# Loading the scale columns of the modulation first and computing two 512-token projection jobs inside the modulation's load

## What is computed

```python
sh_x, sc_x, gt_x = split(silu(c) @ w_ada + b_ada, 3)        # 2048 wide each
sh_c, sc_c, gt_c = split(silu(c_ctx) @ w_ada + b_ada, 3)
h_x = rms_norm(x, norm_g) * (1 + sc_x) + sh_x               # 256 tokens
h_c = rms_norm(ctx, norm_g) * (1 + sc_c) + sh_c             # 256 context tokens
px = h_x @ w_in ;  pc = h_c @ w_in                          # 2048 x 6976
```

## Time and profile before

| | |
|---|---|
| median of 3 runs | 2210.15 us (2209.24 to 2214.47) |
| profiled execution, own time | 2212.03 us, its span 2210.2 us |
| PE busy | 2169.6 us, 98% of the span |
| PEld busy | 1797.2 us, 81% |
| DVE / ACT busy | 1422.2 us / 999.0 us |
| DMA | 409.23 MB, mean 185 GB/s |
| first tile of the first job starts / its eighth ends | 53.34 us / 133.25 us |

### The profile page before, as it was taken

How to read it: one execution, slowest core, us unless ns; L and a number is a source line. 1 busy time by engine, 2 the same in 40 slices (tenths; PEclk the granted TensorE clock), 3 DMA queues, 4 the chain that set the end, 5 groups by cost and what they waited for, 6 DMA issues and landing times.

```text
span 2210.2 us, 29923 instructions
## 1 busy us (share of the span) xinstructions
PE 2169.6 (98%) x11250; PEld 1797.2 (81%) x11250; DVE 1422.2 (64%) x2126; ACT 999.0 (45%) x1486; POOL 105.3 (5%) x124
## 2 busy tenths in 40 slices
PE   5999999999999999999999999999999999999999
PEld 1587888897778888888778888888888888888887
DVE  2257665646846676787788545687778787654455
ACT  3243233434545444555466445544444444344453
POOL 1020100102110120000000000000000000000000
PEclk8999999999999999999999999999999999999999
DMA  9976665543045666665413565666656666656674
GB/s 372 382 231 203 204 212 182 166 121 103 10 169 174 210 202 192 178 186 173 149 39 95 179 192 182 212 190 187 191 181 191 187 190 190 204 190 190 190 242 165
DMA packets 209908, 409.23 MB, mean 185 GB/s; under 512 B 15501, under 2 KB 24069, under 8 KB 208264
## 3 DMA queue, kind: packets, MB, share of 16 engines
q1 hardware_dynamic: 205536, 386.71, 55.3%
q0 software_dynamic: 3360, 16.76, 2.6%
q10 hardware_dynamic: 904, 4.29, 0.5%
HBM read 400.49 MB, written 7.22 MB: 184 GB/s over the span
## 4 chain that ended last, share of the span: by engine, by line
PE 89%; DVE 5%; DMA 3%; ACT 1%; issue 1%; POOL 0%; SPq 0%; DVEq 0%; ACTq 0%
PE bank L2088 52%; PE bank L2098 19%; PE bank L2104 10%; DMA ada_ring<-in_w_ada 2%; PE bank L2216 1%; PE bank L2328 1%; PE bank L2315 1%; PE bank L2274 1%; DVE wlo L1286 1%; PE bank L2240 1%; DMA raw<-in_w_out 1%; PE bank L2225 1%; PE bank L2506 0%; DVE st L1492 0%; DMA raw<-in_w_in 0%
## 5 line engine op out<-in xcount | busy, mean ns | idle before, releaser
L2088 PE MATMUL bank<-whi,xhl 128*128 128x512 f32 (+2 forms) x3776 | 1136.8, 383 | 4.7 <-DVE wlo L1286 3.0
L1286 DVE TENSOR_TENSOR wlo<-raw,whi 128x1024 fp32r<-128x1024 f32 (+2 forms) x649 | 773.1, 1204 | 465.1 <-ACT whi L776 443.6
L776 ACT ACTIVATE whi<-raw 128x1024 fp32r<-128x1024 f32 (+2 forms) x649 | 664.1, 1047 | 671.2 <-PE bank L2088 345.6
L2088 PEld LDWEIGHTS bank<-whi,xhl 128*128 128x128 f32 x3776 | 695.5, 188 | 141.9 <-DVE wlo L1286 6.6
L2088 PE MATMUL bank<-wlo,xhl 128*128 128x512 f32 (+2 forms) x1888 | 719.8, 381 | 0.0
L2098 PE MATMUL bank<-xhl,whi 128*128 128x512 f32 x1792 | 449.1, 392 | 0.0
L2088 PEld LDWEIGHTS bank<-wlo,xhl 128*128 128x128 f32 x1888 | 354.4, 188 | 67.3
L2098 PEld LDWEIGHTS bank<-xhl,whi 128*128 128x128 f32 x1792 | 322.3, 189 | 58.0 <-issue 0.3
L2104 PEld LDWEIGHTS bank<-xhl,wlo 128*128 128x128 f32 x1792 | 244.5, 190 | 17.5
L2104 PE MATMUL bank<-xhl,wlo 128*128 128x256 f32 x1792 | 249.9, 282 | 0.0
L1949 DVE TENSOR_TENSOR up_x<-bank,up_x 128x256 f32<-128x256 f32 x88 | 31.2, 417 | 70.8 <-ACT up_x L783 70.8
(11 more groups left out here) (363 smaller groups left out, 1386.2 us busy)
## 6 DMA issues: line engine op xcount, KB each, us to landing
raw<-in_w_in SPq DMA_DIRECT2D x216, 512.0 KB, 4.0
raw<-in_w_up SPq DMA_DIRECT2D x176, 512.0 KB, 3.7
raw<-in_w_out SPq DMA_DIRECT2D x96, 512.0 KB, 4.7
raw<-in_w_down SPq DMA_DIRECT2D x88, 512.0 KB, 4.5
ada_ring<-in_w_ada SPq DMA_DIRECT2D x64, 512.0 KB, 11.4
gate_w<-in_w_ada SPq DMA_DIRECT2D x32, 512.0 KB, 3.8
raw<-in_w_ple_gate SPq DMA_DIRECT2D x32, 512.0 KB, 4.9
raw<-in_w_in SPq DMA_DIRECT2D x16, 384.0 KB, 4.1
```

The lines of the kernel that those rows point to most:

```text
L776: nc.scalar.activation(whi[:, slot, 0:size], raw[:, slot, 0:size], ACT.Copy).then_inc(hi_ready, 1)
L1286: tt_(wlo[:, slot, 0:size], raw[:, slot, 0:size], whi[:, slot, 0:size].bitcast(F32), ALU.subtract).then_inc(lo_ready, 1)
L2088: ins = mm(b4[tt][:, 0:width], x[:, o:o + P], w, start=k == 0 and i == 0, stop=k == last and i == 2)
```

## The change

The modulation load runs in a new order: all 32 scale tiles first, then shift quarters 0 and 1, two tiles "v", shift quarter 2, two "v", shift quarter 3, four "v": 72 tiles instead of 64. The eight v tiles are the `w_in` tiles of the first job once more, multiplied by the shift columns (`SH32`), so that shift @ w_in of that job comes out as a row. The first job, now columns 2560 to 3071, runs on x with scale only. Later its row is spread over 128 partitions by two matmuls (`L2409`) and added to the job's output by DVE (`add_shift`). The second job, columns 2048 to 2559, is also a 512-token job: its eight tiles run inside the shift's load, after XH and XL have been rebuilt with the shift (`shift_sum` and `shift_low` on DVE, `shift` on ACT). Both jobs use banks 0 to 3. The former first job is now the fifth. `ada_ring` has 10 slots instead of 11. Gate tiles, mixers and the table of relative positions move with the jobs; the first gate load waits for all modulation tiles to be used.

```diff
-JOBS1 = [(512, 512, 4, 0), (0, 512, 2, None), (1024, 512, 2, None),
-         (1536, 512, 2, None), (2048, 512, 4, 512), (2560, 512, 4, 1024), (3072, 512, 2, None),
+JOBS1 = [(2560, 512, 4, 1024), (2048, 512, 4, 512), (0, 512, 2, None), (1024, 512, 2, None),
+         (512, 512, 4, 0), (1536, 512, 2, None), (3072, 512, 2, None),
...
+        ADA_SEQ = ([("scale", i, g) for i in range(4) for g in range(8)]
+                   + [("shift", i, g) for i in range(2) for g in range(8)] + [("v", 0, 0), ("v", 0, 1)]
+                   + [("shift", 2, g) for g in range(8)] + [("v", 0, 2), ("v", 0, 3)]
+                   + [("shift", 3, g) for g in range(8)] + [("v", 0, g) for g in range(4, 8)])
+        IN1_LOAD = {n: k for k, n in enumerate((6, 8, 14, 16, 22, 24, 30, 32, 37, 41, 46, 50, 55, 59, 64, 68))}
+        IN1_TILE = {11: (0,), 19: (2,), 27: (4,), 35: (6,), 69: (14,), 71: (15,)}
...
-        GATE_AT = {n: (g,) for g, n in enumerate([10, 12, 14, 16] + list(range(32, 48)) + [56, 58, 60, 62]
-                                                 + list(range(64, 72)))}
+        GATE_AT = {n: (g,) for g, n in enumerate([17, 18, 19, 21, 23, 25, 27, 28, 29, 31] + list(range(32, 40))
+                                                 + [52, 54, 56, 61] + list(range(64, 74)))}
-        QKV_JOBS = {1: "A", 4: "B", 8: "C"}
-        GATE_JOBS = {2: "A", 6: "B", 9: "C"}
+        QKV_JOBS = {4: "A", 6: "B", 8: "C"}
+        GATE_JOBS = {5: "A", 7: "B", 9: "C"}
...
             def load_gate(g):
+                if g == 0:
+                    sp.wait_ge(ada_used, N_ADA)
...
+            def shift_sum(k):
+
+                dve.wait_ge(tile_used, k // 2 + 1)
+                dve.wait_ge(xl_ready, k + 1)
+                if k >= 2:
+                    dve.wait_ge(sh_lo, k - 1)
+                tt_(TMP[:, k % 2, :], XH[:, 512 * k:512 * k + 512].bitcast(F32), XL[:, 512 * k:512 * k + 512].bitcast(F32),
+                    ALU.add).then_inc(sh_sum, 1)
...
+            def add_shift():
+
+                c, w, nt, pc = JOBS1[0]
+                dve.wait_ge(s_vb, 1)
+                dve.wait_ge(evac, J_IN1 + 1)
+                for tt in range(nt):
+                    x = PX[:, tt, c:c + w] if tt < NT else PC[:, tt - NT, pc:pc + w]
+                    ins = tt_(x, x, bank[7 - tt // NT][:, :], ALU.add)
+                ins.then_inc(s_vadd, 1)
...
             for n in range(N_ADA):
-                j, slot = n // 8, n % ADA_RING
-                if n % 8 == 0 and j >= 1:
+                part, i, g = ADA_SEQ[n]
+                slot = n % ADA_RING
+                j = i + (4 if part == "shift" else 0)
+                if part != "v" and g == 0 and j >= 1:
                     pe.wait_ge(evac, j)
+                if part == "v":
+                    pe.wait_ge(s_bb, 5 + g // 2)
...
-                for k in X_TURN.get(n, ()):
-                    if k == 0:
+                if part == "scale" and g in (5, 6):
+                    if n == 5:
                         pe.wait_ge(xn_ready, 1)
-                    one_round(R_X, k)
-                if n in MOD_COLS:
-                    mod_columns(MOD_COLS[n])
+                    one_round(R_X, 4 * i + g - 5)
+                if n in (8, 16, 24, 32, 9, 17, 25, 33):
+                    one_round(R_X, 4 * (n // 8 - 1) + 2 + n % 8)
+                if n + 1 in ADA_END:
+                    if j >= 5:
+                        in1_tile(8 + 2 * (j - 5))
+                    mod_columns(j)
+                    if 1 <= j < 5:
+                        in1_tile(2 * j - 1)
+                    if j >= 5:
+                        in1_tile(9 + 2 * (j - 5))
...
+            for n in range(16, 24):
+                if n == 16:
+                    pe.wait_ge(s_vr, 1)
+                    for w in range(2):
+                        ins = mm(bank[7 - w][:, :], SEL[:, w:w + 1].to_broadcast([P, P]), MOD[0][:, :], start=True,
+                                 stop=True)
+                    ins.then_inc(s_vb, 1)
                 in1_tile(n)
```

More of the change, by code:

```diff
@@ L598, in load_gate @@
                                  "(k p) n -> p k n", p=P)).then_inc(gw_in[g % 2], 16)
-            for n in range(6, N_KV):
+            for n in range(16, N_KV):
                 jj, g = IN1_ORDER[n]
@@ L906, in _, with mod_rows, shift @@
-            split(6)
-            act.wait_ge(s_bb, 4)
-            one_round(R_X, 12)
-            one_round(R_X, 13)
-            split(7)
-            one_round(R_X, 14)
-            one_round(R_X, 15)
-            split(8)
+            def mod_rows(j):
+                act.wait_ge(ada_used, ADA_END[j])
+                if j >= 3:
+                    act.wait_ge(s_modc, j - 2)
+                copy(MOD[j % 3][:, :], bank[4][:, :]).then_inc(evac, 1)
+            def shift(k):
+                act.wait_ge(sh_sum, k + 1)
+                for w in range(2):
+                    c = 256 * w
+                    ins = nc.scalar.activation(XH[:, 512 * k + c:512 * k + c + 256], TMP[:, k % 2, c:c + 256],
+                                               ACT.Identity, bias=BB[:, k, w:w + 1])
+                ins.then_inc(sh_hi, 1)
@@ new lines, in copy_banks @@
+            def copy_banks(j):
+                c, w, nt, pc = JOBS1[j - J_IN1]
+                act.wait_ge(tile_used, 8 * (j - J_IN1 + 1))
+                for tt in range(nt):
+                    dst = PX[:, tt, c:c + w] if tt < NT else PC[:, tt - NT, pc:pc + w]
+                    copy(dst, bank[tt][:, 0:w]).then_inc(banks_out, 1)
+                act.wait_ge(banks_out, 4 * (j - J_IN1 + 1))
+            for j in range(4):
+                mod_rows(j)
+                split(2 * j)
+                act.wait_ge(s_bb, j + 1)
+                one_round(R_X, 4 * j)
+                one_round(R_X, 4 * j + 1)
+                split(2 * j + 1)
+                one_round(R_X, 4 * j + 2)
+                one_round(R_X, 4 * j + 3)
@@ new lines, in _ @@
+            for j in range(4, 8):
+                k = 4 * (j - 4)
+                mod_rows(j)
+                split(2 * j)
+                shift(k)
+                shift(k + 1)
+                split(2 * j + 1)
+                shift(k + 2)
+                if j == 4:
+                    copy_banks(J_IN1)
+                shift(k + 3)
+            act.sem_inc(evac, 1)
+            act.wait_ge(ada_used, N_ADA)
+            act.wait_ge(s_modc, 8)
+            copy(MOD[0][:, :], bank[6][:, :]).then_inc(s_vr, 1)
@@ new lines, in _ @@
+            for j in range(4):
+                mod_columns(j)
+                split(2 * j)
+                one_round(R_X, 4 * j)
+                one_round(R_X, 4 * j + 1)
+                split(2 * j + 1)
+                one_round(R_X, 4 * j + 2)
+                one_round(R_X, 4 * j + 3)
+            for j in range(4, 8):
+                k = 4 * (j - 4)
+                mod_columns(j)
+                split(2 * j)
+                shift_sum(k)
+                shift_sum(k + 1)
+                shift_low(k)
+                shift_sum(k + 2)
+                shift_low(k + 1)
+                split(2 * j + 1)
+                shift_sum(k + 3)
+                shift_low(k + 2)
+                shift_low(k + 3)
@@ L2077, in tile, with token_major @@
                 body().then_inc(tile_used, 1)
-            def token_major(b4, nt, t, k0, last, stride, base, width, slot, xh=XH, xl=XL, c0=0):
+            def token_major(b4, nt, t, k0, last, stride, base, width, slot, xh=XH, xl=XL, c0=0, ahead=None):
                 for c in range(c0, t):
```

169 lines of the change are left out of this document (85 added, 84 removed).

## The result

The changed kernel takes 2236.39 us (median of 4 runs, 2234.71 to 2240.14), the kernel before 2210.92 beside it: a ratio of 1.0114, 95% interval [1.0102, 1.0126], or 25 us slower. The forecast was 2219.6 with a range to 2227. The sign was right and the size was not. The profiled execution has a span of 2232.9 us, 22.7 more than before; all that follows is about these 22.7. One timed execution among those of the experiments, of e6_gates_by_pool, ran in a slow state (2754.9 us at a granted clock of 0.743) and is left out of that kernel's time and ratio.

The account below looks back on a forecast made before the run. Loads were taken to bound the kernel to about 50 us and PE from then on. Terms -10.9 + 15.1 + 1.7 + 3.6 = +9.5 us on the median 2210.15 gave 2219.6 us, range 2212.5 to 2227.

Parts of the forecast that it names:

- Step 1: Start of the first `w_in` tile, T0: at 42.4 us instead of 53.34, a gain of 10.9 us.
- clock term: Before T0: PE comes back at half clock after standing for the normalized context, which adds 2.3 us.
- Step 2: T0 to the end of T15: PE's work sums to 139.0 us against 123.9 before, +15.1 us.
- loads would not hold this stretch up: T0 to T15: the last load lands some 45 us before use; shift blocks load 16.3 us against 16.5 of PE.
- Rival (c): T0 to T15: loads pace PE after all, so the time is about 2183 us, or 2201; chance 0.08.
- (a): No stand at T20 and T21, or no slow clock: 2213.8 to 2217 us; chance 0.24.
- Step 4: T16 to T23: raw loads queue on SP behind a waiting gate load; PE stands at T20 and T21, +3.6 us.
- the landing: Load of tile 20: lands at about 17 us from T15's start, gate tile 0 ending at 11.5.
- The stand of 2.7 that I had at T21: At T21: PE wants the tile at 21.9 us from T15's start, DVE's split ends at 24.7.
- rival (b): More stands: half clock into T0, lagging shift blocks, DVE in mixers B and C; 2222.5 to 2231 us; chance 0.17.
- Step 5: Mixers' work on DVE beside the later tiles, A as before and B beside tiles 58 to 67: 0, up to 2 us.
- Step 3: Ahead of T16: the row's two fp32 matmuls on PE at 0.86 us each, +1.7 us.

Follow-up runs that it names:

- e6_gates_by_pool: Changed kernel with the loads of gate tiles 0 to 9 issued by GpSimd instead of SP: 2236.54 us, ratio 1.0112.
- e2: Changed kernel with the ten gate tiles at tiles 17 to 31 moved to tiles 32 to 39 (two each), 40 and 41: 2281.0 us, ratio 1.0306.
- e1: Changed kernel with GpSimd's zeroing of px and its loads of the relative position table held back until tile 24 is used: 2237.64 us, ratio 1.0119.
- e3: Changed kernel without the row (no v tiles, spreading matmuls or additions), so its output lacks the first job's shift part: 2229.32 us, ratio 1.008.
- e7: Changed kernel with the eighth and ninth jobs exchanged and the 14 later gate tiles moved with them: 2239.12 us, ratio 1.0126.
- e9: Changed kernel with only gate tiles moved: the first after tile 21 instead of 17, four more among tiles 48 to 62: 2234.4 us, ratio 1.0109.
- e8: Changed kernel with scale rounds in pairs, gate loads 0 to 23 by GpSimd, eighth and ninth jobs exchanged, gate tiles moved: 2217.54 us, ratio 1.0025.
- e10: As e8, gate tiles after 19, 21, ..., 31, two each after 32 to 37, one each after 38, 39, 50, 52, 54, 56 to 63: 2211.91 us.
- e12: As e8, gate tiles after 21, 23, ..., 31, two each after 32 to 38, one each after 39, 56 to 63, 72 to 74: 2210.82 us.

## Why the prediction was right in sign and short in size

At equal work, with the prediction's terms:

| step | predicted | measured in the profiled run |
|---|---|---|
| 1, T0's start | -10.9 (42.4) | -11.4 (53.34 - 41.98) |
| 2, T0 to the end of T15 | +15.1 (139.0) | +18.5 (183.89 - 41.98 = 141.9) |
| 3, the row's two matmuls | +1.7 | +1.3 (183.89 to 185.21) |
| 4, stands from T16 to T39 | +3.6 | +10.3 (98.6 - 87.0 - 1.3) |
| 5, mixers' work on DVE, from T40 | 0 | +4.3 (137.2 - 130.6 - 2.3) |
| sum | +9.5 | +23.0 (22.7 at the end) |

**Step 1** was right in its total. Its clock term was partly luck. In the changed kernel's profiled run the full clock is back by 34 us; in that of e6, whose program is the same up to T15, it goes back to 0.50 behind the second stand and T0 starts at 45.40. Windows of the changed kernel, PE alone (length, busy, clock, DMA share, GB/s):

```profile
29.00:34.00 5.00, 4.51 (x16) 0.58 1.05 387
34.00:37.00 3.00, 2.21 (x14) 1.00 1.06 388
...
40.00:44.00 4.00, 4.00 (x25) 1.00 1.05 387
```

And of e6:

```profile
34.00:37.00 3.00, 2.21 (x12) 0.85 1.05 387
...
40.00:44.00 4.00, 4.00 (x16) 0.50 1.05 387
```

So the first 40 us of this program end 3.4 us apart from one execution to another, on the same work. e2 started T0 late too (45.44); e1, e3, e7 and e9 between 41.75 and 42.30. By the Trainium skill ("TensorE: Matmul & The Clock Gate", Part 1) the length of the throttled stretch varies from run to run for the same kernel; these rows agree. The median lies 2.8 us further from before than the profiled span does. That some of the timed runs had the late start is likely, but they have no trace.

**Step 2** was sized too low by 3.4 us, in three small prices. A `w_in` tile took 5.66 to 5.67 (171.65 to 177.32) and not 5.6: 1.1 over 16 tiles. The eight pairs of modulation tiles that stand alone took 1.00 and not 0.89: 0.9. Column matmuls took 0.95 and not 0.86: 0.6. Another 0.5 is that before had its 16 tiles done at 176.7 (176.97 less the 0.26 by which the copy follows) and not 177.2, and 0.3 is spread. That loads would not hold this stretch up was right: PE waited once, 0.24 us. Rival (c), that the loads pace PE, fell; so did the cheaper (a), since the stand at T20 and the slow clock came.

**Step 4** named the mechanism, the place and the tiles, and e9 shows it: with the first gate tile at 21, the loss from T16 to T23 is gone. The term was mis-sized in two factors. The first is the landing: I had it 5.5 us behind gate tile 0 and it came 9.2 behind it. 3.0 of these are the tables' packets (8.69 against 5.67 in e1), and without them the estimate would have been short by 0.6. The second is the clock: I priced a stand as its length, while behind 5.58 us of stand PE runs at half clock. The twelve matmuls of T20 take 5.3 us (202.27 to 207.56, where T21 starts) in place of 2.72, which costs 2.6 more. The stand of 2.7 that I had at T21 did not come by itself; DVE ended its split only near 207.4, late as forecast, but PE was still at T20. The start of T21 on PE, and the one stand of the next job:

```profile
207.56 0.71 PE L2178 MATMUL bank<-whi,xhl 128*128 128x512 f32 x2
...
233.34 0.73 PE L2178 MATMUL bank<-whi,xhl 128*128 128x512 f32 x2 [1.04 <-DVE wlo L1331]
```

In all 5.6 (stand), 2.6 (clock), 1.0 (the second stand) and 0.6 (T16 to T19 take 11.5 us from 185.21 in place of 10.9) make 9.8 of the 10.3. The result lies beyond the upper end of rival (b), more stands, to which I gave 0.17. Of the places that (b) named, a half clock that lasts into T0 came only in e2 and e6, and no shift block lagged; DVE's part beside the mixers came, and larger.

**Step 5** failed outright: "I put 0, up to 2". I counted B's demand (3.7 us a tile on three tiles) against a lead of three tiles, and called A the same as before. What I didn't add up is the stretch as a whole. Before, 24 of 32 gate tiles lay beside 512-token tiles, where PE takes 5.44 us and split and gate tile 2.73, and B's head work began there too. The change puts a second of the four long jobs into the modulation load, where no gate tile can lie, since the first gate load waits for all modulation tiles. So 16 of 32 now lie beside short tiles, ten of them in T16 to T31 and two in T72 to T79, and A's head work, B's and four gate tiles all stand between T40 and T63, of which T48 to T63 fill DVE to 43.25 us for 43.5 us of PE's work. Of the 6.6 us that T40 to T79 lose in the changed kernel, 3.7 lie in T48 to T63, where head work came to gate tiles that were there before (14.3 us more of it), and 2.1 in T72 to T79, where two gate tiles came to head work that was there before (without them e8 and e10 lose nothing there). e7 and e9 to e12 moved gate tiles among the short jobs, and the loss moved with them; in e8, with none beside a short tile from T40 on, T48 to T79 lose nothing (T40 to T47 lose 4.1, by a late gate load). That A was the same as before was nearly right: 2.5 us in T40 to T55 here, 1.9 there.

**Step 3** was right (1.3 for 1.7). The additions, counted in step 4, cost 0.9 in their job (e3).

What stays open: how much of the 2.8 us by which the median lies further off than the profiled run is the clock at T0; the last 0.5 us of step 4; and how much of the loss of T48 to T63 would stay if the gate tiles went away and B's head work stayed beside short tiles, since no kernel did only that (e9 added four gate tiles there and lost 5.5 us more).

## What to carry to other kernels

Before moving long work elsewhere, ask what was hiding beside it: sum each engine's work over the stretch that is left behind, not per tile. PE's work changed by a few us here; the larger half of the loss came from DVE work and loads that lost their cover.

An issue that waits blocks its whole queue. A load whose slot depends on the engine that the next loads feed makes a closed loop; count how many ring slots lie between it and the wait, and put it behind the loads that PE needs next (with the first gate tile at 21 in place of 17, T16 to T23 won 8 us here, and the extreme of it, e2, cost 50).

A stand of PE costs more than its length if the clock falls with it; and a landing time taken from the whole span (4.0 us here) is too low where a wait makes loads bunch up (5.67 in e1) or small packets run beside them (8.69).
